# The chain of a norm reordered: additions to x ahead, squares behind, and a first chunk in two halves

## What is computed

```python
def rmsnorm(x, g):
    xf = x.astype(F32)
    y = xf * lax.rsqrt(jnp.mean(xf * xf, axis=-1, keepdims=True) + RMS_EPS)
    return (y * g.astype(F32)).astype(x.dtype)

def reference(x, norm_g, ...):
    for i in range(DEPTH):
        g = norm_g[i]
        h = rmsnorm(x, g[0])
        ...
        x = x + rmsnorm(mix, g[1])
        h = rmsnorm(x, g[2])
        x = x + rmsnorm(conv_ffn(h, ...), g[3])
    return x
```

## Time and profile before

| | |
|---|---|
| median of 3 runs | 2267.7 us (2261.79 to 2271.3) |
| the profiled execution, its own time | 2263.93 us |
| its span | 2262.2 us |
| TensorE busy | 2173.0 us, 96% of the span |
| VectorE busy | 1353.5 us, 60% |
| ScalarE busy | 1083.9 us, 48% |
| weights and all other transfers | 381.12 MB, mean 168 GB/s |

### The profile page before, as it was taken

How to read it: one execution, slowest core, us unless ns; L and a number is a source line. 1 busy time by engine, 2 the same in 40 slices (tenths; PEclk the granted TensorE clock), 3 DMA queues, 4 the chain that set the end, 5 groups by cost and what they waited for, 6 DMA issues and landing times.

```text
span 2262.2 us, 34176 instructions
## 1 busy us (share of the span) xinstructions
PE 2173.0 (96%) x11553; PEld 1805.5 (80%) x11553; DVE 1353.5 (60%) x2081; ACT 1083.9 (48%) x1639; POOL 249.2 (11%) x395
## 2 busy tenths in 40 slices
PE   8999989999999999998989998989999999999998
PEld 7777778888888888886776666768888888888886
DVE  7655567676767644445765444457766666664444
ACT  6766454444444443444455555445444444443443
POOL 3341000000000000003004554000000000000000
PEclk9999999999999999998999999999999999999999
DMA  6435545655565665553562222535555555665553
GB/s 211 136 116 177 177 139 170 202 182 194 174 201 178 192 208 191 186 188 110 189 222 66 74 74 81 172 129 186 187 184 193 178 195 176 197 209 189 186 187 129
DMA packets 107194, 381.12 MB, mean 168 GB/s; under 512 B 14114, under 2 KB 14578, under 8 KB 106482
## 3 DMA queue, kind: packets, MB, share of 16 engines
q1 hardware_dynamic: 104962, 373.69, 50.4%
q10 hardware_dynamic: 2160, 6.46, 0.7%
HBM read 377.97 MB, written 2.14 MB: 168 GB/s over the span
## 4 chain that ended last, share of the span: by engine, by line
PE 88%; DVE 6%; ACT 2%; issue 2%; POOL 1%; DMA 1%; DVEq 0%; ACTq 0%; POOLq 0%; SPq 0%
PE set L535 35%; PE set L603 29%; PE set L539 17%; DVE wlo L1266 2%; PE set L700 2%; PE set L682 1%; PE set L724 1%; PE set L627 1%; DVE scored L1524 1%; ACT whi L906 1%; DVE x_sb L1431 1%; POOL probs L490 1%; PE set L684 1%; DMA raw<-in_stream 0%; PE set L717 0%
## 5 line engine op out<-in xcount | busy, mean ns | idle before, releaser
L535 PE MATMUL set<-hs,whi 128*128 128x512 f32 x3584 | 1220.8, 403 | 20.4 <-DVE wlo L1266 7.6
L1266 DVE TENSOR_TENSOR wlo<-raw,whi 128x1024 fp32r<-128x1024 f32 x704 | 858.1, 1229 | 577.5 <-ACT whi L906 576.8
L906 ACT ACTIVATE whi<-raw 128x1024 fp32r<-128x1024 f32 x704 | 738.5, 1057 | 766.2 <-PE set L539 404.8
L539 PE MATMUL set<-hs,wlo 128*128 128x256 f32 x3584 | 856.2, 282 | 0.0
L539 PEld LDWEIGHTS set<-hs,wlo 128*128 128x128 f32 x3584 | 675.7, 191 | 78.6
L535 PEld LDWEIGHTS set<-hs,whi 128*128 128x128 f32 x3584 | 624.0, 191 | 119.4 <-issue 19.1
L603 PE MATMUL set<-whi,hid 128*128 128x512 f32 x1408 | 386.9, 395 | 0.0
L603 PEld LDWEIGHTS set<-whi,hid 128*128 128x128 f32 x1408 | 264.6, 188 | 63.5 <-DVE wlo L1266 0.6
L603 PE MATMUL set<-wlo,hid 128*128 128x512 f32 x704 | 222.5, 395 | 0.0
L603 PEld LDWEIGHTS set<-wlo,hid 128*128 128x128 f32 x704 | 132.4, 188 | 31.7
L603 PE MATMUL set<-whi,os 128*128 128x512 f32 x512 | 146.8, 400 | 0.0
(11 more groups left out here) (178 smaller groups left out, 1180.8 us busy)
## 6 DMA issues: line engine op xcount, KB each, us to landing
raw<-in_stream SPq DMA_DIRECT2D x704, 512.0 KB, 3.4
gain_rows<-rows ACTq DMA_DIRECT2D x4, 1024.0 KB, 5.2
xT<-in_x SPq DMA_DIRECT2D x8, 256.0 KB, 7.9
out_y<-out_f SPq DMA_DIRECT2D x3, 512.0 KB, 2.6
bo_rows<-rows ACTq DMA_DIRECT2D x1, 1024.0 KB, 7.9
wg_raw<-in_w_gates ACTq DMA_DIRECT2D x1, 768.0 KB, 4.4
out_y<-out_f SPq DMA_DIRECT2D x2, 256.0 KB, 2.4
w2k_sb<-in_w ACTq DMA_DIRECT2D x2, 128.0 KB, 5.2
```

Source lines behind the costliest of these rows:

```text
L535: return mm(sets[set_of(u)][:, t, 0:2 * w], whi[:, slot, cols], r, start=first, stop=final)
L539: return mm(sets[set_of(u)][:, t, w:2 * w], wlo[:, slot, cols], r[:, 0:w], start=False, stop=False)
L906: A(whi[:, slot, :], raw[:, slot, :], ACT.Copy).then_inc(hi_ready, 1)
L1266: V.tensor_tensor(wlo[:, slot, :], raw[:, slot, :], whi[:, slot, :].bitcast(F32), ALU.subtract).then_inc(lo_ready, 1)
```

## The change

The first chunk of a norm is cut into two halves of 128 features, each with a semaphore of its own on every link of the chain; the second half is transposed into bank 2. The transposes of chunk 1 move from ahead of chunk 0 to its middle. On VectorE the additions for chunks 2 and 3, 4 and 5, 6 and 7 move forward by one link each, ahead of splits of weights; on ScalarE the squares move behind the split of the same chunk and are made after the high parts of chunks 2, 3, 4 and 5, where they were made after 2, 3, 5 and 6; the sum of the squares, the root and the diagonal are made one link earlier. No computation is added or left out.

```diff
+        def turn_bank(c, kt):
+            return 2 if c == 0 and kt == 1 else c % 2
@@ TensorE, turn_x
+                elif n < 4 and c == 0:
+                    pe.wait_ge(x_half, n)
                 else:
                     pe.wait_ge(x_ready, CH * n + c + 1)
                 for kt in range(CK):
                     for t in range(TT):
+                        if kt == 1 and t == 0 and c == 0 and 1 <= n < 4:
+                            ins.then_inc(x_half_turned, 1)
+                            pe.wait_ge(x_ready, CH * n + 1)
@@ TensorE, h_waits, and what the first unit now calls at each tile
                 def waits(c):
+                    if n > 0 and c == 0:
+                        pe.wait_ge(h_half, n)
+                        return
+            def mid_chunk(n):
+                def before(tile):
+                    if tile == CK:
+                        turn_x(n, 1)
+                        pe.wait_ge(h_ready, h_before(n) + 1)
+                return before
-                unit(ff, hs, waits=h_waits(n))
+                unit(ff, hs, waits=h_waits(n), tile_before=mid_chunk(n))
@@ ScalarE, prenorm
                     high_of_h(n, gain, c)
-                    if c in (2, 3, 5, 6):
-                        square_x(n, (2, 3, 5, 6).index(c))
                     if 1 <= c <= 5:
                         split(g0 + c + RING - 2)
-                take_root(2 * n)
+                    if 2 <= c <= 5:
+                        square_x(n, c - 2)
+                    if c == 6:
+                        take_root(2 * n)
@@ VectorE, norms
-                add_y(0, 1, x_ready, 1)
-                add_y(1, 2, x_ready, 1)
+                add_y(0, 1, x_half, 1, slice(0, P))
+                add_y(0, 1, x_ready, 1, slice(P, FC))
                 last_y()
                 low_of_h(n + 1, gain, 0)
+                add_y(1, 2, x_ready, 1)
+                add_y(2, 4, x_ready, 2)
                 low_of_h(n + 1, gain, 1)
-                for c in range(2, CH):
-                    if c % 2 == 0:
-                        add_y(c, c + 2, x_ready, 2)
-                    if c == 2:
-                        split(g0 + RING - 1)
-                    low_of_h(n + 1, gain, c)
-                    if c < 6:
-                        split(g0 + c + 2)
-                token_r(sq_x, x_squared, 8 * (n + 2), 2 * n + 2)
+                split(g0 + 3)
+                low_of_h(n + 1, gain, 2)
+                add_y(4, 6, x_ready, 2)
+                split(g0 + 4)
+                low_of_h(n + 1, gain, 3)
+                add_y(6, 8, x_ready, 2)
+                split(g0 + 5)
+                low_of_h(n + 1, gain, 4)
+                split(g0 + 6)
+                low_of_h(n + 1, gain, 5)
+                split(g0 + 7)
+                token_sum(sq_x, x_squared, 8 * (n + 2))
+                low_of_h(n + 1, gain, 6)
+                token_inverse(2 * n + 2)
                 make_diag()
+                low_of_h(n + 1, gain, 7)
```

More of the change, by code:

```diff
@@ L256, in build_program @@
         prepared = sem("prepared")
+        x_half, x_half_turned, h_hi_half, h_half = sem("x_half"), sem("x_half_turned"), sem("h_hi_half"), sem("h_half")
         x_ready, x_turned, h_hi_ready, h_ready = sem("x_ready"), sem("x_turned"), sem("h_hi_ready"), sem("h_ready")
@@ L624, in turn_x @@
                         else:
-                            o = norm_banks[n][:, c % UT if n == 4 else c % 2, kt * S + t * P:kt * S + (t + 1) * P]
+                            o = norm_banks[n][:, c % UT if n == 4 else turn_bank(c, kt), kt * S + t * P:kt * S + (t + 1) * P]
                             src = x_sb[:, c, t, kt * P:(kt + 1) * P]
@@ L846, in _ @@
                     turn_x(n, 0)
-                    unit(KC1, hs, waits=h_waits(n))
+                    unit(KC1, hs, waits=h_waits(n), tile_before=mid_chunk(n))
                     spread_r(n)
@@ L964, in high_of_h @@
             def high_of_h(n, gain, c):
-                act.wait_ge(x_turned, CH * n + c + 1)
+                if c == 0:
+                    act.wait_ge(x_half_turned, n)
+                else:
+                    act.wait_ge(x_turned, CH * n + c + 1)
                 for kt in range(CK):
-                    ins = A(hs[:, c * CK + kt, 0:S], norm_banks[n][:, c % 2, kt * S:(kt + 1) * S], ACT.Copy,
+                    if c == 0 and kt == 1:
+                        ins.then_inc(h_hi_half, 1)
+                        act.wait_ge(x_turned, CH * n + 1)
+                    ins = A(hs[:, c * CK + kt, 0:S], norm_banks[n][:, turn_bank(c, kt), kt * S:(kt + 1) * S], ACT.Copy,
                             scale=g_sb[:, gain, c * CK + kt:c * CK + kt + 1])
@@ L1296, in add_halves, with token_sum, token_inverse @@
                     ins.then_inc(evacuated, 1)
-            def token_r(squares, squared, value, k):
+            def token_sum(squares, squared, value):
                 dve.wait_ge(squared, value)
                 V.tensor_reduce(sq_total[:], squares[:], mybir.AxisListType.X, ALU.add).then_inc(total_sq, 1)
+            def token_inverse(k):
                 dve.wait_ge(root_ready, k + 1)
@@ L1304, in token_r @@
                 dve.wait_ge(r_ready, k + 1)
+            def token_r(squares, squared, value, k):
+                token_sum(squares, squared, value)
+                token_inverse(k)
             def low_of_h(n, gain, c):
-                dve.wait_ge(h_hi_ready, h_before(n) + c + 1)
+                dve.wait_ge(*((h_hi_half, n) if c == 0 else (h_hi_ready, h_before(n) + c + 1)))
                 for kt in range(CK):
+                    if c == 0 and kt == 1:
+                        ins.then_inc(h_half, 1)
+                        dve.wait_ge(h_hi_ready, h_before(n) + 1)
                     k = c * CK + kt
-                    ins = V.scalar_tensor_tensor(hs[:, k, S:2 * S], norm_banks[n][:, c % 2, kt * S:(kt + 1) * S],
+                    ins = V.scalar_tensor_tensor(hs[:, k, S:2 * S], norm_banks[n][:, turn_bank(c, kt), kt * S:(kt + 1) * S],
                                                  g_sb[:, gain, k:k + 1], hs[:, k, 0:S].bitcast(F32),
@@ L1426, in y_evac, with add_y @@
                 return evac
-            def add_y(lo, hi, done, by):
+            def add_y(lo, hi, done, by, f=slice(0, FC)):
                 for t in range(TT):
-                    ins = V.scalar_tensor_tensor(x_sb[:, lo:hi, t, :], y[:, lo:hi, t, :], r_token[:, t:t + 1],
-                                                 x_sb[:, lo:hi, t, :], ALU.mult, ALU.add)
+                    ins = V.scalar_tensor_tensor(x_sb[:, lo:hi, t, f], y[:, lo:hi, t, f], r_token[:, t:t + 1],
+                                                 x_sb[:, lo:hi, t, f], ALU.mult, ALU.add)
                 ins.then_inc(done, by)
```

## The result

The changed kernel takes 2236.53 us (median of 4 runs, 2233.86 to 2236.98) against 2265.31 (4 runs, 2261.79 to 2271.3) of the kernel before on the same chip: a ratio of 0.9875 with a 95% interval of 0.9862 to 0.9889, 28.8 us less. The forecast was 2239 with 27.0 less. The two profiled executions, 2263.93 and 2233.86, lie 30.1 apart.

The account below looks back on a forecast made before the run. TensorE, busy 96% of the span, was taken as the bound. Gains of 22.8 (first matmul to spreading), 3.7 (starts) and 0.5 (`rnorm`) made 27.0 us less: 2239 from 2266.2, own range 2231 to 2250, two in ten outside 2230 to 2253.

Parts of the forecast that it names:

- The stops: Two TensorE waits of 2.86 us in the first norm, transposes waiting for additions to x; both go, none replaces them.
- The stretch: From a norm's first matmul to its spreading: 27.75 us per norm, against 34.11, 37.50 and 34.41 before.
- the late `h` of chunk 1: New TensorE wait because chunk 1's transposes move into chunk 0: 0 to 0.5 us, taken as 0.4 per norm.
- The clock's term: Lower clock for 3.5 us from each norm's first matmul: costs 1.75 us a norm, bounds 1.35 to 2.95.
- The start: First addition to first matmul takes 2.4 us with the first chunk halved: gains 1.5, 1.1, 1.1, together 3.7 us.
- A half addition: A 128-column addition on VectorE in the first chunk: 0.28 us, bounds 0.21 and 0.42.
- The end: Sum, root and diagonal come a chunk earlier, so `rnorm` is no longer late: 0.5 us for three norms.
- The sum: Gains of 22.8 us from first matmul to spreading, 3.7 at the norms' starts and 0.5 for `rnorm`: 27.0 us less.
- the stop that moves: Rival, chance 0.13: VectorE's lateness adds up over chunks 1 to 3, one stop stays in each norm: 2252 us.
- the later clock: Rival, chance 0.09: matmuls start earlier but full clock doesn't; lower level lasts 5.9 us in each norm: 2244.5 us.
- rival 3: Chance 0.09: the clock rises later, with 5.9 us at the lower level in each norm, costing 2.95 us: 2244.5 us.

Follow-up runs that it names:

- additions-alone run: Kernel before with only VectorE's additions for chunks 2 to 7 moved one low part earlier, ahead of the weight split: 2241.56 us, ratio 0.9882.
- squares-alone run: Kernel before with only ScalarE's squares moved behind the weight split of the same chunk: 2251.57 us, ratio 0.9924.
- fill runs: Changed kernel with dummy products ahead of each norm's first transposes: 28, 20 and 20 of them took 2236.88 us; 13, 9 and 9 took 2230.44 us.
- short fill: Changed kernel with 13, 9 and 9 dummy products ahead of the three norms' first transposes: 2230.44 us, beside 2234.09 for the changed kernel.
- halves-alone run: Changed kernel with additions from chunk 2 on, squares, sum and root as in the kernel before, keeping only the halves: 2266.65 us, ratio 1.0001.

## Why the prediction was right

**The stops.** Forecast: both go in each norm and none replaces them. Measured: no idle time in the three stretches. The additions-alone run shows the cause, the squares-alone run the size of ScalarE's share (1.2 of 2.86 us).

**The stretch.** Forecast 25.6 + 0.4 + 1.75 = 27.75 us; measured 27.77, 27.48 (1056.76 - 1029.28) and 25.95 in the first profile, 28.1 on average in the second, 26.8 in the third. The fill runs give the length at full clock, 25.95: 0.35 more than seven chunks at 3.26 and one at 2.79, where I had 0.4 for the late `h` of chunk 1. Of the 0.35 some 0.23 are that wait (in the short fill's first norm 0.59 us, 284.74 - 284.15, from chunk 2's transposes to chunk 1's first matmul, where 0.36 is usual). The clock's term is 0 to 2.6 us a norm, 1.4 in the mean of nine stretches, against my 1.75. In the first profile it was 3.3 for the three (81.2 - 3 x 25.95) against 5.25: that is the 2 us by which the sum was short there. That the third norm of two profiles has no stretch at the lower clock at all is luck: I had 2.7 us as the least. I also had the lower clock behind one stop of the kernel before, where it stands behind four of six; the sum doesn't suffer, since it takes the stretches before as measured.

**The start.** Forecast gains of 1.5, 1.1 and 1.1; measured 1.45 (280.60 - 278.09 = 2.51 instead of 3.96), 1.38 (2.49 instead of 3.87) and 1.18 (2.31 instead of 3.49): 4.0 for 3.7. The second gained more since of the 0.4 us that its additions lose, which I had let stay, only 0.17 stayed (1.31 for four against 1.14). A half addition takes 0.27 us from start to start (four from 278.09 to 279.15), for 0.28 forecast. The advice of the Trainium skill (VectorE: DVE Perf Modes, on the TRN2 errata) against short tiles holds in this trace, since half the columns take 0.27 of 0.40 us (before: four from 278.14 to 279.73); the estimate of 0.19 from its table was not reached. The first matmul comes earlier nevertheless.

The step that failed is in what this term rests on. I priced the halves by themselves, and the expectation of the halves-alone run said 4 us: it gained nothing. By the rows of that run the halves make the low part of chunk 1 late, and the addition for chunks 2 and 3 behind it stops TensorE for 3.6 us in three norms; the prediction has no such term. In the changed kernel that addition stands ahead of the low part, so the sum came out; as a sum of independent parts it was wrong.

**The end.** The wait for `rnorm`, 0.5 us for three, is gone as forecast.

**The sum.** 24.8 from the stretches, 4.0 from the starts and 0.5 from `rnorm` are 29.3 of the 30.1 us between the two profiled executions. The other 0.8 I did not trace. Of the rivals, the stop that moves did appear, in the halves alone, and the later clock appeared by chance in two norms of the second profile of the changed kernel (28.4 and 28.5 us), where it cost 2.5 us a norm against the 2.95 of rival 3. Its mechanism by the Trainium skill (TensorE: Matmul & The Clock Gate, Part 4), transposes that don't count as busy, was not tested: the dummy products were plain products, and no run here parts the two.

## What to carry to other kernels

A stop of the engine that bounds a kernel is to be followed to the queue in which its releaser stands, not to the releaser's duration: a pair of additions of 0.7 us each cost 2.86 because it was written behind a split that TensorE needed two chunks later. Where parts of a change feed one queue, price them together: cutting the first chunk in half made new stops of 3.6 us by itself, nearly as much as it won, and with the next addition moved ahead it made none. A stop can cost more than its length: four of six stops of 2.86 us were followed by 3 to 6 us at the lower clock. A kernel whose main engine stands still for 2 to 3 us at a few places can fill them with work that nobody reads, if that ends just before the wait does; it kept the clock up here in six of six places, and the time that it saves was not shown apart from the noise.

## What the runs showed of the hardware

The lower clock followed some idle gaps of 2.3 to 3.5 us and not others of the same program: the changed kernel's third norm ran its first chunk at 1.00 in two profiles and at the lower level in one. Of the 30 norm starts in the ten profiles without a fill, 28 had the lower clock before or in the first chunk; of the six with a fill, none. Stops of 1.65 us never brought it (none of six), stops of 2.86 to 2.91 us did in four of six in the kernel before and in five of six with the halves alone. A product of 128 fp32 columns is two instructions in the trace and 0.23 us at full clock, 3.06 us for 26 instructions.
